# A two-layer fp32 trunk step on one core: modulation units moved into the norms and the MLP, one weight ring for both layers, groups of three units behind each norm, and rotation on the vector engine

## The reference, cut to what matters

```python
mod = silu(cond) @ w_ada + b_ada              # sh1, sc1, g1, sh2, sc2, g2
h = rms(x, g_norm1) * (1 + sc1) + sh1
u = h @ w_in                                   # 32 blocks of gates, 13 of mixers
# pooling, differential attention, Fourier mixing, latent attention -> 4 branches
# both attentions rotate queries and keys of the latent tokens:
#   x1, x2 -> x1*cos - x2*sin, x1*sin + x2*cos
merged = sum(sigmoid(gates) * (branches @ w_branch))
x = x + g1 * (merged @ w_out)
h2 = rms(x, g_norm2) * (1 + sc2) + sh2
x = x + g2 * ((silu(gate) * val) @ w_down)     # gate, val = conv3(h2 @ w_up)
```

## Time and profile before

| | us |
|---|---|
| median of three runs (lowest, highest) | 1367.85 (1366.03, 1370.43) |
| the profiled execution | 1368.89 |
| its span, first to last instruction | 1367.1 |
| PE busy in it | 1309.1 (96%) |
| DVE, ACT, POOL busy | 740.8, 599.6, 82.0 |
| mean granted clock of TensorE | 0.985 |

### The profile page before, as it was taken

How to read it: one execution, slowest core, us unless ns; L and a number is a source line. 1 busy time by engine, 2 the same in 40 slices (tenths; PEclk the granted TensorE clock), 3 DMA queues, 4 the chain that set the end, 5 groups by cost and what they waited for, 6 DMA issues and landing times.

```text
span 1367.1 us, 19336 instructions
## 1 busy us (share of the span) xinstructions
PE 1309.1 (96%) x7832; PEld 1205.6 (88%) x7832; DVE 740.8 (54%) x1260; ACT 599.6 (44%) x1000; POOL 82.0 (6%) x77
## 2 busy tenths in 40 slices
PE   3899999999999999999989999999999899999999
PEld 1887978888889999999979788788898799999999
DVE  0525256444857777764353442664466677777532
ACT  2445544543345444443333554545433544444321
POOL 1000000000710000000100000000044100000000
PEclk9899999999999999999999999999999999999999
DMA  9531244454242333347644222444443233333343
GB/s 372 210 123 57 77 153 171 155 179 167 102 150 98 125 123 125 125 153 270 221 191 139 88 77 76 171 170 170 170 155 104 105 134 126 124 126 125 129 139 124
DMA packets 53545, 198.13 MB, mean 145 GB/s; under 512 B 6416, under 2 KB 6832, under 8 KB 52944
## 3 DMA queue, kind: packets, MB, share of 16 engines
q1 hardware_dynamic: 53136, 196.19, 40.3%
q0 software_dynamic: 320, 0.69, 0.2%
HBM read 194.59 MB, written 2.27 MB: 144 GB/s over the span
## 4 chain that ended last, share of the span: by engine, by line
PE 84%; DVE 7%; ACT 2%; DMA 2%; POOL 2%; issue 1%; SPq 1%; POOLq 0%; DVEq 0%; ACTq 0%
PE bank L1045 24%; PE bank L1046 23%; PE bank L1047 23%; PE bank L1029 3%; DVE w_lo L735 2%; DMA w_raw<-stream 2%; DVE wide L955 1%; PE bank L1260 1%; PE bank L1280 1%; PE bank L1250 1%; SPq L307 1%; ACT w_hi L436 1%; ACT wide L436 1%; DVE act_lo L784 1%; DVE wide L778 1%
## 5 line engine op out<-in xcount | busy, mean ns | idle before, releaser
L735 DVE TENSOR_TENSOR w_lo<-w_raw,w_hi 128x1024 fp32r<-128x1024 f32 x258 | 318.7, 1236 | 368.5 <-ACT w_hi L436 368.2
L1045 PE MATMUL bank<-act_hi,w_hi 128*128 128x386 f32 x1424 | 496.4, 349 | 13.5 <-DVE act_lo L784 12.2
L1047 PE MATMUL bank<-act_hi,w_lo 128*128 128x386 f32 x1424 | 485.8, 341 | 0.0
L1046 PE MATMUL bank<-act_lo,w_hi 128*128 128x386 f32 x1392 | 475.2, 341 | 0.0
L436 ACT ACTIVATE w_hi<-w_raw 128x1024 fp32r<-128x1024 f32 x258 | 271.1, 1052 | 158.7 <-DMA w_raw<-stream 152.6
L1045 PEld LDWEIGHTS bank<-act_hi,w_hi 128*128 128x128 f32 x1424 | 272.1, 191 | 27.2 <-issue 24.5
L1047 PEld LDWEIGHTS bank<-act_hi,w_lo 128*128 128x128 f32 x1424 | 271.7, 191 | 0.0
L1046 PEld LDWEIGHTS bank<-act_lo,w_hi 128*128 128x128 f32 x1392 | 266.6, 191 | 1.0
L1045 PE MATMUL bank<-mlp_hi,w_hi 128*128 128x386 f32 x352 | 119.2, 339 | 0.0
L1046 PE MATMUL bank<-mlp_lo,w_hi 128*128 128x386 f32 x352 | 119.1, 338 | 0.0
L1047 PE MATMUL bank<-mlp_hi,w_lo 128*128 128x386 f32 x352 | 118.9, 338 | 0.0
(11 more groups left out here) (202 smaller groups left out, 1420.2 us busy)
## 6 DMA issues: line engine op xcount, KB each, us to landing
w_raw<-stream SPq DMA_DIRECT2D x258, 512.0 KB, 3.3
ada<-ada_w SPq DMA_DIRECT2D x68, 512.0 KB, 3.3
ada_head_a<-ada_w SPq DMA_DIRECT2D x16, 512.0 KB, 5.3
ada_head_b<-ada_w SPq DMA_DIRECT2D x12, 512.0 KB, 8.7
time_consts<-time_consts SPq DMA_DIRECT2D x2, 1920.0 KB, 15.8
params<-params SPq DMA_DIRECT2D x2, 926.0 KB, 11.3
x<-x_in SPq DMA_DIRECT2D x1, 1544.0 KB, 9.9
y_out<-x SPq DMA_DIRECT2D x1, 1158.0 KB, 6.6
```

The source lines that it names most:

```text
L735: V.tensor_tensor(wlo[s][:, :], raw[s][:, :], whi[s][:, :].bitcast(F32), ALU.subtract).then_inc(lo_ready, 1)
L1045: T.matmul(out, wb[s][0][:, w, :], hi[k], start=first and k == 0, stop=False)
L1046: T.matmul(out, wb[s][0][:, w, :], lo[k], start=False, stop=False)
L1047: ins = T.matmul(out, wb[s][1][:, w, :], hi[k], start=False, stop=last and k == n - 1)
```

## The change

1. Modulation: each layer's 48 units are cut into six sums q of 8 units (`ADA_ORDER`, `CHUNK`; q = 0 is the scale and q = 1 the shift of the first norm, q = 5 the last gate). Layer 0 keeps 16 units at the start, has 24 in its attention steps and 8 behind the square sums of the second norm. Layer 1's units: 8 in layer 0's up projection, 8 between blocks of its down projection, 8 behind the square sums of layer 1's first norm (`hole_units`), 16 in layer 1's attention, 8 behind the second norm. The 8 of each second norm (`norm_ada`) and the 8 of the hole have buffers of their own, so they are loaded ahead. The others go through the ring of two.
2. One weight stream: the slot of a unit is its number over both layers modulo 4. Units 0 to 3 of layer 1 are loaded, and units 0 to 2 split, during the end of layer 0.
3. `group` takes the place of `pair` behind each norm: three units, 9 matmuls per block for blocks 0 to 3 and 6 for blocks 4 to 7, then the third unit's last 12. In layer 0 ACT and DVE split all three before the norm's blocks.
4. Rotation: the matmuls L1139 and L1288 go; DVE makes the rotated copy by a shuffle within 32 partitions (`stream_shuffle`), with the sign in the sine table.
5. Attention on PE: scores(i), then turn(i-2), then the gate; weigh in odd steps. turn(23) and weigh(23) lie inside the first branch block. The sub-norm's sums move from step 13 to 16.
6. `merge_sum` has four buffers; POOL's block d waits for `merged_lo` of block d-4. ACT's squares in the output projection come before the split of the same round.

```diff
+ADA_ORDER = ([(0, q, k) for q in range(6) for k in range(KD)]
+             + [(1, 0, k) for k in range(KD)]
+             + [(1, q, k) for q in (1, 2) for k in range(4)]
+             + [(1, q, k) for q in (1, 2) for k in range(4, KD)]
+             + [(1, q, k) for q in range(3, 6) for k in range(KD)])
+ATTN_ADA = (HEAD, 72)
+NORM_ADA = (40, 88)
+UP_ADA, DOWN_ADA, HOLE_ADA = 48, 56, 64
+RING = [*range(16, 40), *range(48, 64), *range(72, 88)]
+ADA_STEP = ([2, 2, 1, 1, 1, 1, 0] + [1] * 8 + [0] + [1] * 8, [1, 0] * 8 + [1] * 8)
...
-    ms_t, ms_end = tile("merge_sum", 2 * TOK, val_at)
+    ms_t, ms_end = tile("merge_sum", 4 * TOK, val_at)
...
+                sp.wait_ge(gated_ready, FROM + (l + 1) * KD * 4)
+                for n in range(KD):
+                    load_norm_ada(l, n)
...
-                    if d >= 2:
-                        pool.wait_ge(mrg_lo, l * KD + d - 1)
+                    if d >= 4:
+                        pool.wait_ge(mrg_lo, l * KD + d - 3)
...
+                    if n == 0 and l == 0:
+                        for u in range(3):
+                            split(u)
+                    if n == 0:
+                        act.wait_ge(shift_ready, l + 1)
...
-                    split(O0 + d + 2)
                     if d in (3, 5, 7):
                         act.wait_ge(x1_ready, FROM + l * KD + d - 1)
                         square(d - 3)
+                    split(O0 + d + 2)
...
+                        if k == 0 and n == 0 and l > 0:
+                            modulation(l, 1)
...
-                    own(V.tensor_tensor(tmp, bank[6][NOPE:QKW, :].rearrange("p (b t) -> p b t", b=2),
-                                        cc("sin", NOPE, QKW).unsqueeze(1).to_broadcast([ROPE, 2, LAT]), ALU.mult))
+                    own(V.stream_shuffle(tmp, xs, ROTATE))
+                    own.wait()
+                    own(V.tensor_tensor(tmp, tmp, cc("sin", NOPE, QKW).unsqueeze(1).to_broadcast([ROPE, 2, LAT]), ALU.mult))
...
+                def group(u, wait):
+                    half = KD // 2
+                    for q in range(3):
+                        unit_ready(u + q)
+                    for k in range(KD):
+                        wait(k)
+                        for q in range(3 if k < half else 2):
+                            ins = dense(bank[q][:, 0:TOK], u + q, [k], HI[k:k + 1], LO[k:k + 1], k == 0, k == KD - 1)
+                            if k == KD - 1:
+                                ins.then_inc(unit_done, 1)
+                    dense(bank[2][:, 0:TOK], u + 2, range(half, KD), HI[half:], LO[half:], first=False).then_inc(unit_done, 1)
...
-                    if i >= 1:
-                        turn(i - 1)
...
                     scores(i)
-                    if i + 1 in ROPE_STEPS:
-                        rotate(ROPE_STEPS.index(i + 1))
-                    if i == 13:
+                    if i >= 2:
+                        turn(i - 2)
+                    if i == 16:
...
                     gate(PREP_GATES + i)
-                    if i >= 2 and i % 2 == 0:
-                        weigh(i - 1)
+                    if i >= 3 and i % 2 == 1:
+                        weigh(i - 2)
...
+                    if (d, n) == (0, 0):
+                        turn(STEPS - 1)
+                    if (d, n) == (0, 2):
                         weigh(STEPS - 1)
...
                 square_sums(1)
-                ada_units(HEAD + sum(ADA_STEP) + ADA_TAIL, ADA_E)
+                norm_units(l)
-                pair(P0, (0, 1), HI, LO, lambda k: pe.wait_ge(norm_lo, (l * 2 + 1) * KD + k + 1))
+                group(P0, lambda k: pe.wait_ge(norm_lo, (l * 2 + 1) * KD + k + 1))
...
+                    if l < DEPTH - 1 and 1 <= i < 1 + KD:
+                        ring_ada(UP_ADA + i - 1, UP_ADA + i)
...
+                        at = i * 4 + d
+                        if l < DEPTH - 1 and at < KD - 1:
+                            ring_ada(DOWN_ADA + at, DOWN_ADA + (KD if at == KD - 2 else at + 1))
```

More of the change, by code:

```diff
@@ L94 @@
 PW = _n
-CCOL = {n: (i * P, (i + 1) * P) for i, n in enumerate(("ones", "ident", "ones32", "ones64", "rot"))}
-CCOL["dft"] = (5 * P, 7 * P)
-CCOL["cos"] = (7 * P, 9 * P)
-CCOL["sin"] = (9 * P, 11 * P)
-CW = 11 * P
+CCOL = {n: (i * P, (i + 1) * P) for i, n in enumerate(("ones", "ident", "ones32", "ones64"))}
+CCOL["dft"] = (4 * P, 6 * P)
+CCOL["cos"] = (6 * P, 8 * P)
+CCOL["sin"] = (8 * P, 10 * P)
+CW = 10 * P
+ROTATE = [j ^ 8 for j in range(32)]
 TP_C, TP_L = 0, 4 * CTX
@@ L122, in wait @@
     def wait(self, but=0):
-        self.eng.wait_ge(self.sem, self.layer * self.per + self.n - but)
+        self.eng.wait_ge(self.sem, self.n - but)
 def program(nc, stream, ada_w, params, caches, consts, time_consts, x_in, cond,
@@ L763, in norm @@
                     scale, shift = (sc1, mod[:, 0:8, :]) if n == 0 else (sc2, mod[:, 24:32, :])
-                    if n == 0:
-                        split(0)
-                        split(1)
-                        dve.wait_ge(head_par_loaded, 16 * l + 16)
-                        modulation(0, 0, 16)
+                    if n == 0 and l == 0:
+                        dve.wait_ge(head_par_loaded, 16)
+                        dve.wait_ge(ada_done, HEAD)
+                        modulation(0, 0)
+                        modulation(0, 1)
                         scales(sc1, 8, "g1")
-                    if n == 0:
+                    if n == 0 and l == 0:
                         clear_gaps()
+                        for u in range(3):
+                            split(u)
                     own.wait()
@@ L1013, in _ @@
                             split(D0 + u + 3)
+                    if d == KD - 1 and l < DEPTH - 1:
+                        split(UNITS)
+                        split(UNITS + 1)
                     dve.wait_ge(unit_done, FROM + l * UNITS + D0 + 3 * d + 3)
                     residual(d, d % 4, 40, x2_ready)
-                assert own.n == DVE_OWN, own.n
+                if l < DEPTH - 1:
+                    clear_gaps()
+                    split(UNITS + 2)
         @block.tensor
```

329 lines of the change are left out of this document (189 added, 140 removed).

## The result

| | before | changed |
|---|---|---|
| median (lowest, highest), four runs each | 1368.5 (1366.0, 1370.4) | 1346.5 (1344.7, 1347.3) |
| span of the profiled execution | 1367.1 | 1344.6 |
| PE busy | 1309.1 | 1291.9 |
| mean granted clock | 0.985 | 0.992 |

The ratio is 0.9838, 95% interval 0.9819 to 0.9858: 22 us faster. The forecast was 1348.6. The changed kernel run once more beside the last experiments gave 1344.8, ratio 0.9834 (0.9819 to 0.9850).

What follows compares the result with a forecast made beforehand. PE was taken as the bound, so the change sums PE work removed, work moved and holes shrinking or growing: thirteen terms, -19.3 from 1368.9, give 1349.6, or 1348.6 us as median. Range 1342 to 1354 (0.55); 8 in 10 from 1337 to 1360.

Steps and rivals of the forecast that it cites:

- A: Rival: everything has room; units cost 0.57, DVE is never late, merging stall shrinks 1.9 per layer: 1334.3 us, chance 0.18.
- B: Rival: DVE becomes the bound in attention if a shuffle takes 1.42 us: +5.7, 1354.3 us, chance 0.17.
- Parts 1 and 2: Part 1: rotations leave PE, -7.8, -2.4, -1.7. Part 2: attention's waits, sub-norm sums and slow stretches, -3.6, -1.9, -1.6.
- part 3: Modulation units: -8.0 in attention, +12.4 for 16 units at 15 places in layer 0's MLP; net +4.4.
- part 4: DVE in attention: shuffles and moved modulation make scores late near step 8; +3.5 in all (0 to +9).
- The clock term: Slow stretch after attention's first wait, 1.7 lost per layer; half of it taken as gain, -1.6.
- Rival D: Gains not on the path: a DVE or ACT chain behind PE's removed work gives them back; 1364.1 us, chance 0.07.
- Part 5: Second norms: PE starts earlier on preloaded units and doesn't starve; -3.9 in layer 0, -3.1 in layer 1.
- Part 6: First norm of layer 1: PE starts near 702.2 instead of 707.08; -5.2 (-3.5 to -7).
- Part 7: First norm of layer 0: splitting unit 2 before the norm delays PE's start; +2.0 at the end of three units.
- Part 8: Merging: deeper buffers can't gain, weigh(23) comes later; +1.0 per layer, +2.0 in all (-6 to +5).
- Part 9: Weight stream: in the up and down projections weight loads queue behind ring loads for under 1 us; nothing.

Runs made afterwards that it cites:

- the last experiments: Changed kernel with two units at layer 0's start (1343.9 us), MLP modulation units two by two (1344.3), or two units at a time behind each norm (1348.4).
- the shuffle alone: Kernel before with only the rotations by matmul, in both attentions, replaced by the shuffle on DVE: 1363.5 us, ratio 0.9959.

## Why the prediction was right, point by point

The time (1346.5) lies 2 us below the forecast and far from every rival's (A 12 us below, B 8 above). The steps:

- **Parts 1 and 2** with the attention side of part 3 and part 4 were -21.8 (seven terms: -7.8, -2.4, -3.6, -1.9, -1.6, -8.0, +3.5). Measured: -23.6, of which 0.7 is the two turn(23) moved into the branch stage (weigh(23) stood there before). Late scores took 2.0 more than forecast, so some 3 us of gain are left over that no term names and no row here assigns. The 0.98 of a rotation runs from 190.14, where its row starts, and not from 190.16. The preparation was -1.7, measured -1.37: DVE's `ckv_normed` (0.82 in PE's row at 110.68) is what is late next, as said. The clock term was a sum of two things that were not foreseen singly: both old slow stretches went (-3.4) and one new came, at 868 behind a late score (+1.7).
- **Part 4**: mechanism right, size low. The shuffle is 0.73 to 0.74 in attention, near the 0.71 taken and above the 0.6 of the prediction's other estimate. Late scores are 5.5 us and not 3.5, six of them and not one, the largest (2.02) at the score of step 8 in layer 0, as forecast, but (1.97) at that of step 6 in layer 1. Doubling the shuffle shows the slope: nearly all that is added to DVE there is paid. Rival B's condition (1.42 us) was not met, but its mechanism is what the doubled shuffle shows; it was right to keep it at 0.17.
- **Parts 1 and 4 together**: their forecast is -11.9 + 3.5 = -8.4, and the shuffle alone measured -5.7. Most of the 2.7 between is the low term of part 4: 5.4 us came back in the old order, and 5.5 stand as late scores in the new one. Where DVE's delay shows (at the turns or at the scores) is set by the order; that the order makes it smaller is not shown. Rival D was thus half true of part 1: DVE's chain takes back about half of what the shuffle alone wins in attention.
- **Part 3**: 0.8 per place forecast, 6.19/8 = 0.77 measured; second unit 0.43 forecast and measured. This was read from steps between starts, not from the busy time of 0.64.
- **Part 5**: the start without a DMA wait and the 72 matmuls at full speed came (12.82 against 12.7), the group being worth 1.49 of it. With the clock (0.2 and 3.0) and the fifth unit's wait taken out, both layers gain 2.2 before the first matmul and 1.55 and 0.64 behind it, so -3.7 and -2.8 against -3.9 and -3.1. The output projection before the norm failed a step. "SP waits for the last gate product in front of them, but the slot that its next load needs is freed only later" is true of the queue of issues and was taken for the whole cost. The transfers behind it were not followed: eight times 512 KB, issued from 361 on, were landing until 376, and the next weight load, at 369.26, behind them took 7.9 us instead of 3.2. The term was 0 and measured 1.5 and 1.7 in this trace, some 1.0 per layer over seven executions.
- **Part 6**: forecast start 702.2 and -5.2. The down projection with the hole is +0.47. In it are seven places with eight units, by the prices above 6 x 0.77 + 0.77 + 0.43 = 5.8; so the hole is 5.3 shorter, and with the -1.29 of the three units the gain up to unit 3 is 6.6, or 1.4 more than forecast. Of that 0.8 is the slow stretch behind the hole, which halved (6.8 us at half clock before, 3.4 now, so 1.7 lost where 2.5 was taken), and 0.2 is a slip in the forecast: 717.4 + 0.7 against 723.1 is -5.0 and not -5.2. That stretch is absent in six of twelve profiled executions of the changed kernel and its variants. The order of events is as written: the split ahead of the table load, the load, the shift behind the first block.
- **Part 7**: +2.0 forecast, +2.28 measured at the end of the three units (56.53 against 54.25). The forecast's 38.2 adds up to 38.1, which changes nothing. The first matmul is at 41.68 rather than 40.8, since the load landed 1 us later in that run (40.56 in the next).
- **Part 8**: the sum was +1.0 per layer, measured +0.39, and here a step failed too; the wait for `w_lo` that was to stay at 3 us or more is 2.56. Later start: with two buffers the stage is +1.41 against before, just what was counted (1.5). But the depth was said to have "nobody idle to serve" because DVE is busy for all of 345 to 362. That stretch left out DVE's idle moments on both sides. The one behind it is 1.12 us before the last `w_lo`, for an ACT that stood behind POOL, and the depth, which removes it, is worth 1.02. The one in front, in DVE's timeline of the kernel before, waits for POOL's first sum; the depth leaves it as it is (1.93 at 336.00 in the changed kernel):

```profile
343.44 0.56 DVE L955 SCALAR_TENSOR_TENSOR wide<-gates_a,bank 128x386 f32<-128x386 f32 x1 [1.93 <-POOL merge_sum L429]
```

  The cited rule (the Trainium skill, SBUF — State Buffer, section "SBUF: two separate sides": the pair of ports is an exclusive lock) describes the rows well. DVE's and then POOL's timeline in the changed kernel:

```profile
342.67 1.21 DVE L786 TENSOR_TENSOR w_lo<-w_raw,w_hi 128x1024 fp32r<-128x1024 f32 x1
343.80 1.23 DVE L1007 SCALAR_TENSOR_TENSOR merged_lo<-merge_sum,merged_hi 128x386 fp32r<-128x386 f32 x1
```

```profile
342.82 1.79 POOL L475 TENSOR_TENSOR wide<-wide 128x386 f32<-128x386 f32 x1
344.57 1.19 POOL L476 TENSOR_TENSOR wide<-wide 128x386 f32<-128x386 f32 x1
345.84 1.03 POOL L478 TENSOR_TENSOR merge_sum<-wide 128x386 f32<-128x386 f32 x1
```

  POOL's addition that starts inside DVE's `w_lo` takes 1.79 instead of 0.86, and DVE's `merged_lo`, which takes 0.55 where POOL is idle (347.09 in the kernel before), takes 1.23 behind it. But the inference from rule to price ("so deeper buffers can't gain") was wrong: turns taken one after another bound the rate (4.15 us from `w_lo` to `w_lo`, 4.30 with two buffers, 4.4 forecast), while the gain was in one wait at the end.
- **Part 9**: nothing, as forecast: the rest of layer 1's up projection, without inserted units, is 174.38 against 174.39.

The profiled execution fell by 22.5 us against 19.3 forecast, and the parts miss by more than the total. On the dear side are the fifth unit's wait (+3.2 over both layers) and the late scores (+2.0). On the other side are the full clock in layer 1's output projection (-3.0), which no term named, the hole (-1.4), the branch stage (-1.2) and the 3 us of attention that nothing explains. That these cancel is luck. The clock at that place varies: the other executions of the changed kernel and its variants have a slow stretch there in six of eleven.

What stays open: where the 3 us of attention come from; what turn(i-2) is worth without the rotations on DVE; how much of layer 1's attention gain is order and how much clock, since the two old slow stretches and the new one don't lie at the same places; and why the fifth unit's wait varies from 0 to 2.75 us between executions.

## What to carry to other kernels

Work that moves to a less busy engine is paid for by what waits on that engine in that step, in either order of the steps tried here (2.4 to 3.1 us per layer). What helped was to place it where that engine has no other extras (2.4 and 2.7 us, of which 1.7 in layer 1 is the clock). When loads are put ahead of others in a queue, follow the bytes to their landing and not only the issue. Before calling a chain gap-free, read it from its first instruction to the one that ends the wait, with each queue that this one stands in. Before giving a stage's difference to an edit, compare the granted clock of that stage.

## What the hardware showed that was not expected

- The shuffle within 32 partitions costs the same 0.72 to 0.74 us for 32 and for 128 partitions of 512 elements, and its mask load 0.01 us.
- The same wait does not always bring the slow clock. The late score of 2.0 us at step 8 of layer 0, near 220, was followed by full clock in three of eight profiled executions that have it, by 3.4 us at half clock in three and by 6.8 us in two. The wait of 2.02 us at the start of layer 1 was followed by 3.4 us at half clock in six of twelve. Stretches from the late score on, the changed kernel's first and second profiled execution:

```profile
217.80:230.30 12.50, 10.48 (x78) 9.18 (x71) 9.15 (x21) 6.52 (x15) 0.00 (x0) 1.00 0.45 165
```

```profile
217.50:230.00 12.50, 10.48 (x59) 8.88 (x51) 8.65 (x20) 6.02 (x14) 0.00 (x0) 0.73 0.23 84
```

  A difference of 3 us between two kernels is therefore read by stage first: one such fall is 1.7 or 3.4 us of it.
